# Output projections of a Strassen trunk: M5 taken ahead of M3, M3 accumulated onto V + M5, 28 adds in place of 32

## The reference

```
h = h + y                                      # y ends in o @ w_out (ao) or (u * sv) @ w_out (go)
h = h + swiglu(rms_norm(h, norm_ffn[i]), ...)  # ends in (silu(h @ w_gate) * (h @ w_up)) @ w_down (d0, d1)
```

## Time and profile before

| | us |
|---|---|
| median of 3 runs | 2624.1 (2624.06 to 2625.99) |
| profiled execution | 2624.77 |
| its span, first to last instruction | 2623.0 |
| TensorE busy | 2538.5 (97%) |
| VectorE busy | 1714.5 (65%) |
| GpSimd busy | 1291.0 (49%) |
| ScalarE busy | 1106.5 (42%) |

### The profile page before, as it was taken

The page is one execution under the profiler, slowest core; times in us unless marked ns, Lnnn a source line. Parts: engine busy times, 40 slices in busy tenths (PEclk is TensorE's granted clock), DMA queues, the critical chain, the costliest instruction groups (busy, mean ns, idle before and its releaser), DMA issues.

```text
span 2623.0 us, 33623 instructions
## 1 busy us (share of the span) xinstructions
PE 2538.5 (97%) x11752; PEld 2098.9 (80%) x11752; DVE 1714.5 (65%) x2197; ACT 1106.5 (42%) x1952; POOL 1291.0 (49%) x989
## 2 busy tenths in 40 slices
PE   7998999979999999998999999999998999999998
PEld 6787888768888888887888888888876888888886
DVE  4124657967777866575675899965666778656556
ACT  4124776443333344454433433344543333334444
POOL 3134445545555555445666455545454555555543
PEclk9999999989999999999999999999998999999999
DMA  5674234415666648663788455587633566325864
GB/s 188 212 263 132 65 97 150 147 53 201 213 212 213 228 146 298 193 207 121 272 305 272 137 181 180 169 303 252 208 104 101 202 211 220 122 80 194 275 189 145
DMA packets 305517, 489.30 MB, mean 187 GB/s; under 512 B 32274, under 2 KB 128147, under 8 KB 305364
## 3 DMA queue, kind: packets, MB, share of 16 engines
q1 hardware_dynamic: 305364, 487.32, 55.5%
HBM read 326.15 MB, written 152.70 MB: 183 GB/s over the span
## 4 chain that ended last, share of the span: by engine, by line
PE 84%; issue 5%; POOL 4%; DVE 4%; ACT 2%; DMA 1%; SPq 0%; POOLq 0%; DVEq 0%; ACTq 0%
PE ps L610 27%; PE ps L612 26%; PE ps L611 26%; PE ps L2574 2%; PE ps L2433 1%; POOL ebuf L1175 1%; POOL ebuf L1174 1%; DVE r_all L1764 1%; DVE r_all L1739 1%; DVE xl_all L1746 1%; POOL g_sb L1185 0%; POOL ring_lo L678 0%; DMA stage<-in_a_w_in 0%; ACT ring_hi L674 0%; DVE s_ring L696 0%
## 5 line engine op out<-in xcount | busy, mean ns | idle before, releaser
L678 POOL TENSOR_TENSOR ring_lo<-stg,ring_hi 128x512 fp32r<-128x512 f32 x682 | 970.2, 1425 | 950.6 <-ACT ring_hi L674 950.1
L674 ACT ACTIVATE ring_hi<-stg 128x512 fp32r<-128x512 f32 x682 | 430.4, 631 | 1073.4 <-PE ps L612 1011.3
L610 PE MATMUL ps<-xh_all,ring_hi 128*128 128x512 f32 x1568 | 615.7, 393 | 1.3 <-DVE r_all L2119 0.9
L611 PE MATMUL ps<-xl_all,ring_hi 128*128 128x512 f32 x1568 | 612.2, 390 | 0.0
L612 PE MATMUL ps<-xh_all,ring_lo 128*128 128x512 f32 x1568 | 611.9, 390 | 0.0
L696 DVE TENSOR_TENSOR s_ring<-s_stage,s_ring 128x512 fp32r<-128x512 f32 x242 | 302.7, 1263 | 227.4 <-ACT s_ring L692 227.1
L610 PE MATMUL ps<-ring_hi,s_ring 128*128 128x512 f32 x1064 | 416.0, 391 | 6.2 <-DVE r_all L1764 3.9
L612 PE MATMUL ps<-ring_hi,s_ring 128*128 128x512 f32 x1064 | 414.2, 389 | 0.0
L611 PE MATMUL ps<-ring_lo,s_ring 128*128 128x512 f32 x1064 | 414.0, 389 | 0.0
L610 PEld LDWEIGHTS ps<-xh_all,ring_hi 128*128 128x128 f32 x1568 | 295.9, 189 | 63.9 <-issue 1.8
L612 PEld LDWEIGHTS ps<-xh_all,ring_lo 128*128 128x128 f32 x1568 | 295.5, 188 | 61.8
(11 more groups left out here) (223 smaller groups left out, 3553.0 us busy)
## 6 DMA issues: line engine op xcount, KB each, us to landing
s_stage<-h_scratch SPq DMA_DIRECT2D x238, 256.0 KB, 3.6
stg<-t_scratch SPq DMA_DIRECT2D x200, 256.0 KB, 3.0
h_scratch<-r_all SPq DMA_DIRECT2D x34, 1024.0 KB, 5.1
h_scratch<-r_all SPq DMA_DIRECT2D x80, 256.0 KB, 3.1
stg<-in_w_ffn_gate SPq DMA_DIRECT2D x34, 512.0 KB, 4.4
stg<-in_w_ffn_up SPq DMA_DIRECT2D x34, 512.0 KB, 5.9
stg<-in_w_ffn_down SPq DMA_DIRECT2D x66, 256.0 KB, 3.4
t_scratch<-r_all SPq DMA_DIRECT2D x28, 512.0 KB, 2.9
```

What stands on the lines that cost most here:

```text
L610: pe.matmul(bank, s_hi, m_hi, start=first, stop=False, skip_group_check=more)
L611: pe.matmul(bank, s_hi, m_lo, start=False, stop=False, skip_group_check=more)
L674: nc.scalar.activation(weight_slot(ring_hi, g), weights(g), ACT.Copy).then_inc(wh_done, 1)
L678: nc.gpsimd.tensor_tensor(weight_slot(ring_lo, g), weights(g), f32(weight_slot(ring_hi, g)), ALU.subtract).then_inc(wl_done, 1)
```

## The change

The order of the D phases becomes M1, M2, M6, M5, M3, M7, M4. M6, M5 and M3 run in banks 0 to 3 one after another, M5 accumulating on V and M3 on V + M5. C12 is then V + M5 + M3 in one group of adds, and V + M5 is added once, into C22. That leaves seven groups, 28 adds: M1, M2, V, V + M5 (C22), V + M5 + M3 (C12), M7, and the last. The adds of every product but M1 stand first in the step that follows the product. In front of M6, M5, M3, M7 and M4 TensorE waits bank by bank. The S4 sums of ao stand one step later. All counts of `added` are renumbered; the order of the U and G phases keeps the old ORDER.

```
-ORDER_V = (1, 2, 6, 5, 3, 7, 4)
+ORDER_D = ORDER_V = (1, 2, 6, 5, 3, 7, 4)
...
 def store_resid(d, part):
-                    sp.wait_ge(added, 32 * d + (16, 24, 28)[part] + i + 1)
+                    sp.wait_ge(added, 28 * d + (16, 20, 24)[part] + i + 1)
...
 def square(n, t):
-                wait(act, added, 32 * n + (16 if t < 4 else 24) + t + 1)
+                wait(act, added, 28 * n + (16 if t < 4 else 20) + t + 1)
...
+                if k == 1:
+                    dve.wait_ge(r_ld[0], 64 * (n + 1))
                 if k == 3:
                     dve.wait_ge(r_ld[1], 64 * (n + 1))
+                if k == 6:
+                    dve.wait_ge(added, 28 * n + 16)
+                for t in range(4):
+                    product_done(n, name, k - 1, t)
+                    if k == 1:
+                        add(n, t, 0, t)
+                    if k == 2:
+                        dve.wait_ge(added, 28 * n + t + 1)
+                        add(n, t, 0, 4 + t)
+                    if k == 3:
                         add(n, 4 + t, 0, t)
+                    if k == 4:
+                        add(n, 4 + t, 1, t)
+                    if k == 5:
                         add(n, t, 1, t)
+                    if k == 6:
+                        add(n, 4 + t, 1, 4 + t)
...
 def d_phase(n, name):  (VectorE)
-                    if k == 6 and j == 0:
-                        for t in range(4):
-                            product_done(n, name, 5, t)
-                            add(n, 4 + t, 1, 4 + t)
-                    if name == "ao" and 2 <= k < 6 and j == 0:
+                    if k >= 2 and j == 0:
                         add_product(n, name, k)
                     if name == "ao" and 3 <= i < 3 + AP:
                         ao_sums(i - 3)
-                    if name == "ao" and 3 + AP <= i < 3 + 2 * AP:
-                        ao_s4(i - 3 - AP)
+                    if name == "ao" and 4 + AP <= i < 4 + 2 * AP:
+                        ao_s4(i - 4 - AP)
                     for b in s_cuts_at(g):
                         cut_stationary_lo(dve, b)
                     if k == 1 and j == 0:
-                        dve.wait_ge(r_ld[0], 64 * (n + 1))
-                        for t in range(4):
-                            product_done(n, name, 0, t)
-                            add(n, t, 0, t)
-                    if name != "ao" and 2 <= k < 6 and j == 0:
                         add_product(n, name, k)
-                    if k == 5 and j == 1:
-                        for t in range(4):
-                            add(n, 4 + t, 1, t)
-                        dve.wait_ge(added, 32 * n + 24)
...
 def d_phase(n, name):  (TensorE)
-                for k, q in enumerate(ORDER):
-                    first_bank = 0 if q in (1, 6, 5) else 4
+                for k, q in enumerate(ORDER_D):
+                    first_bank = 0 if q in (1, 6, 5, 3) else 4
...
-                        if j == 0 and q == 6:
-                            pe.wait_ge(added, 32 * n + 4)
-                        if j == 0 and q == 3:
-                            pe.wait_ge(added, 32 * n + 8)
-                        if j == 0 and q == 5:
-                            pe.wait_ge(added, 32 * n + 12)
-                        if j == 0 and q == 7:
-                            pe.wait_ge(added, 32 * n + 16)
...
-                            if j == 0 and q == 4:
-                                pe.wait_ge(added, 32 * n + 24 + t + 1)
+                            if j == 0 and q in (6, 5, 3, 7, 4):
+
+                                pe.wait_ge(added, 28 * n + {6: 0, 5: 8, 3: 12, 7: 4, 4: 20}[q] + t + 1)
```

More of the change, by code:

```diff
@@ L100, in d @@
         n = self.pairs[self.phase[g]]
-        return ORDER[self.place[g] // n], self.place[g] % n
+        return ORDER_D[self.place[g] // n], self.place[g] % n
     def v(self, g):
@@ L1780, in last_add @@
                     product_done(n, name, 6, i)
-                    dve.wait_ge(added, 32 * n + 12)
+                    dve.wait_ge(added, 28 * n + 12)
                     add(n, 4 + i, 0, 4 + i)
@@ L1797, in add_product @@
             def add_product(n, name, k):
-                if k == 2:
-                    for t in range(4):
-                        product_done(n, name, 1, t)
-                        dve.wait_ge(added, 32 * n + t + 1)
-                        add(n, t, 0, 4 + t)
+                if k == 1:
+                    dve.wait_ge(r_ld[0], 64 * (n + 1))
                 if k == 3:
                     dve.wait_ge(r_ld[1], 64 * (n + 1))
-                    for t in range(4):
-                        product_done(n, name, 2, t)
-                        add(n, 4 + t, 0, t)
-                if k == 4:
-                    for t in range(4):
[L1811 to L1816, removed]
+                if k == 6:
[8 more added lines that the diff above has]
+                    if k == 3:
+                        add(n, 4 + t, 0, t)
+                    if k == 4:
+                        add(n, 4 + t, 1, t)
+                    if k == 5:
                         add(n, t, 1, t)
+                    if k == 6:
+                        add(n, 4 + t, 1, 4 + t)
             def d_phase(n, name):
@@ L2424, in turn_op @@
                     pe.wait_ge(n_normed, 8 * n + t + 1)
-                    pe.wait_ge(added, 32 * n + 24)
+                    pe.wait_ge(added, 28 * n + 20)
                 elif op == "A22":
@@ L2465, in d_phase @@
                                 pe.wait_ge(sv_done, 4 * EP)
-                            if j == 0 and q == 4:
-                                pe.wait_ge(added, 32 * n + 24 + t + 1)
+                            if j == 0 and q in (6, 5, 3, 7, 4):
+                                pe.wait_ge(added, 28 * n + {6: 0, 5: 8, 3: 12, 7: 4, 4: 20}[q] + t + 1)
                             mm = product(pe, ps[:, first_bank + t, :], s_slot(g, 0)[:, tile(t)], s_slot(g, 1)[:, tile(t)],
-                                         w_ring(ring_hi, g), w_ring(ring_lo, g), j == 0 and q in (1, 2, 3, 7),
-                                         j == pairs - 1, q in (6, 5, 4))
+                                         w_ring(ring_hi, g), w_ring(ring_lo, g), j == 0 and q in (1, 2, 7),
+                                         j == pairs - 1, q in (6, 5, 3, 4))
                             if j == pairs - 1 and t < 3:
@@ L2492, in u_phase @@
                                 pe.wait_ge(xl_done, 28 * n + ready_before("U", op))
-                                pe.wait_ge(added, 32 * n + (32 if q == 3 else 24))
+                                pe.wait_ge(added, 28 * n + (28 if q == 3 else 20))
                             if q == 1 and s:
@@ L2516, in u_phase @@
                                     if r == 8:
-                                        pe.wait_ge(added, 32 * (n + 1))
+                                        pe.wait_ge(added, 28 * (n + 1))
                                     turn_op(n, "U", r)
```

## The result

The changed kernel takes 2636.93 us (median of 5, 2636.37 to 2638.63), the kernel before in the same comparison 2625.84. The ratio is 1.0046 with a 95% interval of 1.0033 to 1.0058: slower by about 12 us by the ratio, by 11.1 between the two medians. The forecast was 2636.4, that is 12.3 over the 2624.1 from which it was reckoned. The profiled span is 2635.0 us against 2623.0.

The account below looks back on a forecast made before the run. TensorE, busy 97% of 2623.0 us, was taken as the bound. From 2624.8, +5.0 for hand-overs, +7.8 for ao, -0.5 for transposes and -0.7 for the profiled execution gave 2636.4 us; range 2630.0 to 2642.5, forecast band 2632 to 2641.

Parts of the forecast that it names:

- Hand-overs in d0, go and d1: At M6 to M5 and M5 to M3, TensorE waits for the adds: 6 x 0.84 = +5.0 us.
- banks 1 to 3 then keep up: At a hand-over only bank 0 is late, since four adds in 2.47 us are faster than four banks in 2.72.
- The transposes: In d0 and go, transposes start without the 0.24 us wait, twice: -0.5 us.
- M5's start in ao: M5 waits for V's adds behind VectorE's backlog, starting at 486.4 against M3's 479.75: +6.6 us (+3.5 to +10.1).
- worst case on all nine: In ao, all nine VectorE operations before V's adds stretch to 1.8 us each; TensorE would start near 494.
- The clock: After ao's long wait TensorE runs 4.9 us at half speed: +2.4 us (1.5 to 2.5).
- M3 and M4 in ao: In ao, a steady hand-over from M5 to M3, +0.8 us, and a shorter wait at M7 to M4, -0.7 us.
- GpSimd's wait: In ao, the 1.12 us wait at 492.07 goes, with 0.2 of restart: -1.3 us.
- the lower end of the stated range: 2630.0 us: VectorE free of GpSimd in ao, -3.2; bare seams, -0.9; all four adds won at M4, -1.8.
- The hand-overs did not hide: Rival, all four projections: hand-overs hide and only gains are left, 2620.1 us, not slower; chance 7%.
- The seams-only case: Rival: in ao M5 starts where M3 did, leaving the hand-overs' cost, +3.3 us, 2627.4; chance 7%.
- Short waits did not drop the clock: Rival, at each hand-over: waits of 0.7 us drop the clock like long ones, seven at 2.4, 2653 us; chance 2%.

Follow-up runs that it names:

- the fourth experiment: The changed kernel with the adds of M2 to M7 one step earlier on VectorE, in all four projections: 2628.92 us, ratio 1.0016 to the kernel before.
- the second experiment: The kernel before with the change in d0, go and d1 alone, ao keeping the old order, groups and waits: 2630.4 us, ratio 1.0021.
- fifth: The changed kernel with ao's S sums one pair ahead of the cuts on VectorE: 2636.8 us, ratio 1.0041 to the kernel before.
- third experiment: The changed kernel with V's four adds in ao right behind those of M2, step 8 not 12: 2634.44 us, ratio 1.0036 to the kernel before.

## Why the prediction was right, step by step

**Hand-overs in d0, go and d1: right in their number and place, 0.3 too cheap.** 6 x 0.84 = 5.0 was forecast from d1's old M7 to M4. Two errors lie in the 0.84. M5 and M3 start 0.77 late (0.61 of wait, 0.16 of restart), not 0.84: the adds begin at 1824.38, 0.05 before the bank is wanted at 1824.43 (its last matmuls began at 1823.75, and a bank takes 0.68). The old rows had shown just that. In the earlier trace rows the adds begin at 1070.02, but the prediction took the cut's start and duration, which overlaps the add by 0.07. And "banks 1 to 3 then keep up" was wrong: the first step behind the wait takes 2.84 us in place of 2.72 (1825.20 to 1828.04). It takes 2.84 in the kernel before too, behind M3's wait in ao and behind the one for GpSimd's weights, so this belongs to the restart and not to the adds. Together a hand-over costs 0.89, six 5.4.

**The transposes: right, and worth twice the forecast.** Both waits of 0.24 are gone, but d0 and go win 0.48 and 0.45 there, 0.9 in place of 0.5. With it d0, go and d1 come to +4.4, forecast +4.5: two errors that cancel, which is luck.

**M5's start in ao: right in its mechanism, 0.6 short.** Counted from ao's first matmul, M5 starts 7.25 us later than M3 did (42.48 against 35.23), where 6.6 was forecast. The prediction let four operations stretch by 0.75 each, which is 3.0, though its sum has 3.2. Three were stretched by 1.07, to 1.75, and one by 0.69, 3.9 together. The Trainium skill's rule (SBUF — State Buffer, Who interferes with whom), that such a pair excludes each other for a whole instruction, fits these rows better than the mean of a series did. Its worst case on all nine did not come true. GpSimd had six weight cuts to do, from 473.23 to 482.54, and ScalarE's next weight cut waited 9.14 us for the standing TensorE, so GpSimd ran out of work, and VectorE's operations from 483.01 on take 0.68 again.

**The clock: +2.4 forecast, 1.9 measured** by the run that kept TensorE busy.

**M3 and M4 in ao.** M3 starts 8.66 us later than M5 did (56.21 against 47.55). The forecast was 6.6 + 2.4 - 1.3 + 0.8 = 8.5; that it is so close is luck in part, since M5's start was 0.65 too early and the clock 0.5 too dear. At M4, 0.7 was to be won; it was 0.4 (0.64 of wait against 1.03). ao in all: +8.3, forecast +7.8. GpSimd's wait is gone as forecast.

**Not in the prediction:** +0.8 us in f1, +0.1 in f0, -0.8 in the V and gMLP phases and -0.8 ahead of ao, -0.6 in sum, none of which the change touches. The median of the kernel before also moved, from the 2624.1 on record to 2625.84. So that 2636.4 and 2636.93 lie within 0.6 us is luck in part; the difference to the kernel before was forecast as 12.3 and is 12.0 between the profiles and 11.1 between the medians. By the terms given for it, the lower end of the stated range would be 2630.5 and not 2630.0.

**The rivals.** The hand-overs did not hide, though they can be made to (the fourth experiment shows the very order that does it). The seams-only case is what the second experiment measures, and ao's share came on top. Short waits did not drop the clock: over the 5 us behind the hand-over at 1825 the granted clock is 1.00.

## What to carry to other kernels

When a product is made to accumulate in the banks that the product in front has just filled, its start hangs on how soon the reader comes to them. Look in the trace for what the reading engine is doing at that moment: "first in its step" is too late if the step in front ends with an instruction that lasts until the bank is wanted. Putting the reads one step earlier, ahead of work with a lead of five steps, made the hand-over free in the three long projections. Price a wait by when the next step starts, not by the wait alone: here 0.61 of wait cost 0.89. In a short phase look for the reader's backlog too, since the new wait sits behind all of it. And 16 adds taken off an engine with idle time were worth 0.9 us, all of it at the two places where TensorE had waited behind them.

## What the hardware showed that was not expected

The price of the clock's fall did not follow the length of the wait. Over the 5 us behind waits of 8.57, 7.33, 6.68 and 3.64 us (the changed kernel and the fourth, fifth and third experiment) the granted clock is 0.58, 0.50, 0.69 and 0.50, and the steps there take 1.9, 2.8, 1.4 and 2.4 us more than behind a short wait. Waits of 0.6 to 1.4 us left the clock at 1.00. Keeping TensorE on useless transposes through the wait kept the clock up.

The parts that the change does not touch did not stay equal either. Between the profiles of the kernel before and of the mix (new order in the long projections, ao as before), f0 differs by 1.7 us (447.41 and 449.11), all of it within 40 us of its start. The table by stretch for the 25 us that begin 15 us behind f0's first matmul, in these two:

```profile
545.17:570.17 25.00, 16.84 (x69) 13.07 (x70) 18.62 (x24) 9.56 (x16) 10.08 (x8) 0.75 0.14 43
```

```profile
546.27:571.27 25.00, 17.12 (x62) 13.25 (x63) 15.41 (x23) 8.95 (x16) 7.45 (x6) 0.66 0.14 43
```

The granted clock is 0.75 and 0.66. The same stretch of f1 has 0.73 in the kernel before and 0.66 in the changed one, whose f1 is 0.8 us longer. TensorE works in bursts there, and where the lower clock falls among them differs from one execution to the next. That the clock is the whole of these differences is not shown. They are as large as several terms of the sum, so a term under 2 us is read from its own phase and not from the time of the kernel.
